# Down stages of six feed-forward blocks: 512 moving columns on one load of the weights' rounded part

## The reference, cut to what matters

```
g, u = split(h @ w_up)              # w_up: 1024 x 5632
x = x + gate * ((silu(g) * u) @ w_down)   # w_down: 2816 x 1024
```

## Time and profile before

| what | value |
|---|---|
| median of 3 runs | 1592.78 us (1592.54 to 1593.91) |
| the profiled execution, its time | 1593.82 us |
| its span, first to last instruction | 1592.0 us |
| TensorE busy | 1555.1 us, 98% of the span, 13306 products |
| VectorE busy | 1281.9 us, 81% |
| ScalarE busy | 905.5 us, 57% |
| GpSimd busy | 239.9 us, 15% |
| mean granted TensorE clock | 0.997 |
| memory traffic | 252 GB/s over the span |

### The profile page before, as it was taken

The page is one execution under the profiler, slowest core; times in us unless marked ns, Lnnn a source line. Parts: engine busy times, 40 slices in busy tenths (PEclk is TensorE's granted clock), DMA queues, the critical chain, the costliest instruction groups (busy, mean ns, idle before and its releaser), DMA issues.

```text
span 1592.0 us, 32473 instructions
## 1 busy us (share of the span) xinstructions
PE 1555.1 (98%) x13306; PEld 1530.2 (96%) x13306; DVE 1281.9 (81%) x1933; ACT 905.5 (57%) x1563; POOL 239.9 (15%) x254
## 2 busy tenths in 40 slices
PE   3999999999999999999999999999999999999998
PEld 2999999999999999999999999999999999999998
DVE  6788898888788878888888888788888888786553
ACT  5445557764554655458665545667555466664553
POOL 4122000022210122000123221001221010021100
PEclk9999999999999999999999999999999999999999
DMA  9999975459898789864569998534899973457761
GB/s 343 332 334 335 330 271 160 159 189 342 307 318 299 279 310 319 300 235 160 178 222 334 310 339 269 162 128 147 307 337 326 322 238 127 139 192 238 238 214 40
DMA packets 110996, 403.11 MB, mean 253 GB/s; under 512 B 12562, under 2 KB 12818, under 8 KB 110720
## 3 DMA queue, kind: packets, MB, share of 16 engines
q1 hardware_dynamic: 109280, 395.87, 71.8%
q0 software_dynamic: 1568, 5.17, 1.2%
HBM read 399.94 MB, written 1.05 MB: 252 GB/s over the span
## 4 chain that ended last, share of the span: by engine, by line
PE 87%; DVE 8%; ACT 2%; DMA 1%; issue 1%; SPq 0%; DVEq 0%; ACTq 0%
PE PS L559 86%; DVE SCR L1709 2%; DVE WL L1706 2%; DVE SCR L1706 1%; DMA ring<-in_ada 1%; DVE ring L1732 1%; ACT WH L1230 1%; DVE SCR L2063 1%; DVE SMALL L2062 1%; ACT SCR L1517 0%; PE PS L1069 0%; DVE SQ L1709 0%; DVE SMALL L2102 0%; DVE SMALL L2104 0%; DVE SQ L1706 0%
## 5 line engine op out<-in xcount | busy, mean ns | idle before, releaser
L1706 DVE TENSOR_TENSOR WL<-ring,WH 128x1024 fp32r<-128x1024 f32 (+1 forms) x508 | 604.3, 1223 | 186.1 <-ACT WH L1230 185.9
L559 PE MATMUL PS<-HH,WH 128*128 128x256 f32 (+1 forms) x2640 | 627.9, 279 | 4.7 <-ACT WH L1230 4.7
L559 PE MATMUL PS<-HL,WH 128*128 128x256 f32 (+1 forms) x2640 | 615.2, 277 | 0.0
L1230 ACT ACTIVATE WH<-ring 128x1024 fp32r<-128x1024 f32 (+1 forms) x508 | 511.6, 1050 | 46.3 <-PE PS L559 44.7
L559 PEld LDWEIGHTS PS<-HH,WH 128*128 128x128 f32 x2640 | 496.9, 189 | 6.7 <-ACT WH L1230 3.5
L559 PEld LDWEIGHTS PS<-HL,WH 128*128 128x128 f32 x2640 | 491.9, 188 | 0.5
L559 PE MATMUL PS<-HH,WL 128*128 128x256 f32 (+1 forms) x2640 | 375.9, 278 | 0.0
L1732 DVE CUSTOM_DVE_ANT_0 ring<-ring,CB,VC 128x1024 f32<-128x1024 f32 x238 | 331.1, 1408 | 12.0 <-DMA ring<-in_ada 11.9
L559 PEld LDWEIGHTS PS<-HH,WL 128*128 128x128 f32 x2640 | 337.1, 189 | 0.3 <-DVE WL L1706 0.3
L559 PE MATMUL PS<-AH,WH 128*128 128x256 f32 x1056 | 291.9, 276 | 0.0
L559 PE MATMUL PS<-AH,WL 128*128 128x256 f32 x1056 | 291.5, 276 | 0.0
(11 more groups left out here) (215 smaller groups left out, 1456.4 us busy)
## 6 DMA issues: line engine op xcount, KB each, us to landing
ring<-in_up SPq DMA_DIRECT2D x176, 512.0 KB, 5.9
ring<-in_ada SPq DMA_DIRECT2D x144, 512.0 KB, 6.2
ring<-in_ffn SPq DMA_DIRECT2D x132, 512.0 KB, 4.8
ring<-in_mod SPq DMA_DIRECT2D x96, 512.0 KB, 5.8
ring<-in_down SPq DMA_DIRECT2D x88, 512.0 KB, 5.8
ring<-in_win SPq DMA_DIRECT2D x64, 512.0 KB, 5.4
ring<-in_wout SPq DMA_DIRECT2D x32, 512.0 KB, 4.6
ring<-in_winv SPq DMA_DIRECT2D x8, 512.0 KB, 4.6
```

The lines of the kernel that those rows point to most:

```text
L559: return e.matmul(out, lhsT, rhs, start=start, stop=stop, skip_group_check=skip)
L1230: e.activation(half_of(i)[0], slot_of(("half", i, 0))[:, 0:w], ACT.Copy).then_inc(s_hi, 1)
L1706: return e.tensor_tensor(out, a, b, op)
```

## The change

1. AH and AL become one tensor AHL of shape [128, 22, 2, 256], so that for each block k the rounded part and the remainder lie side by side: 512 columns in a row. The names AH and AL are views of it.
2. In the down stages, for chunks 0 to 6, the two products with WH become one with 512 moving columns. It writes all 512 columns of the chunk's bank: WH times AH in columns 0 to 255, WH times AL in columns 256 to 511. The product with WL stays as it was and adds to columns 0 to 255. Chunk 7 keeps its three products.
3. `residual` of chunks 0 to 6 has two steps: first columns 256 to 511, times the gate, are added to X, then columns 0 to 255. The second waits for the first (`step`), and it alone adds 1 to `s_x`.
4. Near the beginning of each down stage products with 4 stationary columns are put in, into bank 6: 1, 2, 4 and 8 of them ahead of the first triple of the first four blocks, and 1 and 2 ahead of the third triple of the last two.

```
-        AH = nc.alloc_sbuf_tensor_at("AH", [128, NF, S], F32R, offset=scr_at)
-        AL = nc.alloc_sbuf_tensor_at("AL", [128, NF, S], F32R, offset=scr_at + 4 * NF * S)
+        AHL = nc.alloc_sbuf_tensor_at("AHL", [128, NF, 2, S], F32R, offset=scr_at)
+        AH, AL = AHL[:, :, 0, :], AHL[:, :, 1, :]
...
                     out = PS[:, down_bank(n, c), 0:256]
-                    mm(out, wh[:, g, :], xh(k), start=k == 0, stop=False)
-                    mm(out, wh[:, g, :], xl(k), start=False, stop=False)
+                    if i == (0, 0, 0, 0, 2, 2)[FFN_AT[n]]:
+                        for _ in range((1, 2, 4, 8, 1, 2)[FFN_AT[n]]):
+                            narrow(PS[:, 6, 0:256], xh(0))
+                    if c < KD - 1:
+                        mm(PS[:, down_bank(n, c), :], wh[:, g, :], AHL[:, k, :, :].rearrange("p a s -> p (a s)"),
+                           start=k == 0, stop=False, skip=True)
+                    else:
+                        mm(out, wh[:, g, :], xh(k), start=k == 0, stop=False)
+                        mm(out, wh[:, g, :], xl(k), start=False, stop=False)
                     if g == 0:
                         e.wait_ge(s_lo, h + 1)
-                    last = mm(out, wl[:, g, :], xh(k), start=False, stop=k == kt - 1)
+                    last = mm(out, wl[:, g, :], xh(k), start=False, stop=k == kt - 1, skip=c < KD - 1)
...
             def residual(n, c):
                 e.wait_ge(*summed(n, c))
-                stt(X[:, c, :], PS[:, down_bank(n, c), 0:256], MOD[:, 24 * n + 16 + c:24 * n + 17 + c], X[:, c, :], ALU.mult,
-                    ALU.add).then_inc(s_x, 1)
+                gate = MOD[:, 24 * n + 16 + c:24 * n + 17 + c]
+                if c < KD - 1:
+                    step(stt(X[:, c, :], PS[:, down_bank(n, c), 256:512], gate, X[:, c, :], ALU.mult, ALU.add))
+                stt(X[:, c, :], PS[:, down_bank(n, c), 0:256], gate, X[:, c, :], ALU.mult, ALU.add).then_inc(s_x, 1)
```

## The result

The changed kernel takes 1609.51 us (median of 4 runs, 1607.74 to 1609.60), against 1593.05 before (4 runs, 1592.54 to 1593.91): ratio 1.0099, 95% interval 1.0087 to 1.0112. It is slower by 16.5 us, outside the predicted range, which ended at 1603.6.

A forecast was written before the change was run, and what follows sets the result against it. TensorE was taken to bound the kernel, its down-stage products starting 113.3 ns apart. Pairs -1.0, added products +2.0 and residual +0.2 sum to +1.2 us on the median 1592.78, giving 1594.0 us, range 1588.3 to 1603.6.

The forecast's parts named there:

- What bounds the kernel: Down stages: TensorE bounds them, products starting 113.3 ns apart with weight loads hidden; VectorE has least room behind it.
- Pairs for triples: Down stages, chunks 0 to 6: 924 triples of 340.0 ns become pairs of 338.9 ns, -1.0 us (-6.2 to +7.1).
- Rival A: Down stages: extra cost comes once per product, wide product 220.0 ns, pair 333.3, total 1588.8 us; chance 0.25.
- Rival B: Down stages: wide product throws TensorE into the 117.7 ns rhythm, pair 347.7, chunk 7 slow too, 1603.6 us; chance 0.33.
- eight short loads in a row end outside it: Second mixer: eight 4-column products are followed by five intervals of 116 ns, taken as a sign for the slow rhythm.
- Rival C: Half 16 in two stages: VectorE comes late, TensorE stalls, then the 117.7 ns rhythm; +1 to +1.5 us; chance 0.07.
- Rival D: Down stages: a 512-column product hardly longer than a 256-column one, each pair saving 113 ns, 1490 us; chance 0.01.
- Added products: Down stages: 18 products with 4 stationary columns at 113 ns each, on TensorE's path, +2.0 us.
- Residual: VectorE in down stages: 42 more additions ahead of WL, tightest at half 16 of the first and fifth stages, +0.2 us.
- Layout: Joining AH and AL in AHL moves no instruction and changes no length, writes hidden under the up stage: nothing.

The follow-up runs named there:

- e6: Kernel before, each triple's WL product in the middle with fewer stationary columns: 4, 32, 64, 96 stay at 113.3 ns; 112 takes 117.8, 120 about 120.
- e7: One wide pair at each down stage's start, 256-column triples behind, 0 to 16 4-column products between: 117.8 ns a product with none, 113.4 with one.
- e3: Changed kernel without the added products, the wide product cut in two of 256 columns: 1595.35 us, kernel before 1593.75, ratio 1.0012.
- e1: Changed kernel without its 18 added 4-column products: 1607.39 us, kernel before 1593.75, ratio 1.0087.
- e2: Kernel before with only the 18 added 4-column products put in: 1595.47 us, kernel before 1593.75, ratio 1.0013.
- e8: Changed kernel with its added products moved ahead of chunk 7 (0, 1, 2, 0, 1, 2 in the six stages): 1606.11 us, one execution.
- e10: Changed kernel without added products, wide product cut in two, residual adding only the bank's lower half in chunks 0 to 6: 1593.43 us, ratio 0.9997.

## Why the prediction was wrong, step by step

- **What bounds the kernel** was right: TensorE, start to start, with hidden loads. Dropping 924 loads brought nothing; so would short loads up to 96 columns (e6).
- **Pairs for triples** is the step that failed. It priced the wide product from two rows behind a break, 230 ns, took 117.7 off for the neighbour and *kept the rhythm*: 225.6, a pair 338.9, and so a term of -1.0 us. Measured: 226 for the first wide product of a stage, and then 234.9 + 118.4 = 353.3 for nearly all others, so the term is +12.3 us. That is 5.6 ns a pair over the top of my bounds, 347.7: in a dense stretch of pairs a wide product takes longer than behind a break, and the neighbour goes at the slow rhythm. That 226 agrees with 225.6 is luck in part. I had taken 117.7, a start-to-start time, off 230, a time from a load's start; the like measure for 256 columns is 115, and with it the sum gives 228.3 and a pair of 341.6. I treated the rhythm as a state that the stage brings along, with a chance of 0.33 that it is lost. The rows with 258 columns had shown that another length has another price while it lasts; e7 shows that a single wide product leaves the 256-column products behind it slow for the rest of the stage.
- **Rival A** (faster, 1588.8): its 220.0, once 6.7 per product, occurs nowhere. The shortest wide products, behind 113.3 ns, take 225 to 226, and the two that one replaces 226.7: even so nothing was to be won. The range began at 1588.3, for which the prediction has no sum; A comes to 1588.8.
- **Rival B** (slower, 1603.6) had the right mechanism and sign: the rhythm is lost in the pairs and in chunk 7 (1.5 us of a forecast 1.7). Its pair was mis-sized, 347.7 for 353.3, which is 5.2 us over 924, and that puts the result outside the range. One of its reasons was misread: "eight short loads in a row end outside it". The mean of 116 over the five intervals hides that the first two are 123 and 119 ns and the others 113 (the kernel before, TensorE):

```profile
724.25 0.28 PE L559 MATMUL PS<-HH,WH 128*128 128x256 f32 x1
...
724.59 0.28 PE L559 MATMUL PS<-HL,WH 128*128 128x256 f32 x1
```

  These are three intervals in 0.34 us, and the quick rhythm goes on behind them. So in the trace before too the 4-column products were followed by the quick rhythm.
- **Rival C**: the stall exists (0.3 us in the first stage), but its slow rhythm behind the stall does not (e3). **Rival D** is out: no product with 512 columns took under 225 ns.
- **Added products**: +2.0 forecast, and 2.0 by the lengths of the stages in e1 and in e2. "What they do for the new length I can't read": nothing for the wide products; they bring back the quick rhythm of the 256-column products where no wide one follows (e7, e8).
- **Residual**: the tightest place was right, the size wrong. I counted one more addition, as if VectorE waited for TensorE long enough at each chunk. In e3 four add up in both stages, less what VectorE had waited ahead of the last one: 1.38 us in the fifth stage, 0.18 in the first, which the prediction took for the same. With pairs at 353.3 ns VectorE had more room and the residual cost 0.3 us, against 0.2 forecast; with triples it costs 1.6 (e3).
- **Layout**: nothing, as forecast (e10).
- The Trainium skill's gap for an isolated product in "TensorE: Matmul & The Clock Gate", Back-to-back issue gap, about 2.5 ns whatever the columns, gave an estimate of 1592.7 here. Measured 1609.5: in float32r with 128 stationary columns no length from 256 to 512 has shown under 6.7 ns, and what is on top jumps with the lengths, so the trace disagrees.

What stays open is the cause of the rhythm itself: why 256 columns with loads of up to 96 or of 128 stationary columns meet well, and 112, 258 or 512 do not. The runs show where the quick rhythm is lost and kept, not its mechanism. It is shown that the length of the products makes the change slow: e3 and e10 undo that length and the slow pairs are gone.

## What to carry to other kernels

Price a merged product by start-to-start times of that very length in a dense stretch, not by a fixed gap; where loads are hidden, fewer of them save nothing. When dense products of one length run faster than others, a single product of another length can cost the rest of the stage 4% (e7), so look for what breaks the rhythm and put a short repair right behind it. Where a step of an engine gets longer, count how many times it runs before its result is needed, and take off only what that engine waited for others on the way: the same four additions cost 1.43 us in one stage and 0.23 in another (e3).

## What the runs showed of the hardware

- Two rhythms for products with 128 stationary and 256 moving columns in float32r at 2.4 GHz: 113.3 and 117.8 ns. Each holds for 500 products and more; one product with 512 columns ends the quick one, one with 4 stationary columns brings it back where only 256 columns follow (e7, e8).
- Pairs with one or two longer products (258 to 512 columns) cost 20 to 40 ns on top of their columns, in a way that depends on both lengths: 8 columns more can be 6.7 ns less (512 + 264 against 512 + 256), and one pair (384 + 256) has two prices, 286.7 and 300, in one stage.
- With 4, 32, 64 or 96 stationary columns in every third product the quick rhythm stays; with 112 the products are 117.8 ns apart and with 120 about 120 (e6, one stage each).
